# Dense tokens of layer 1 placed behind the last expert sum of layer 0

## What is computed

```python
for l in range(2):
    hn = rms_norm(h, norm_mix[l])
    if l == 0: y = gmlp_mix(hn, ...)                  # chunk token mixer
    else:      y = banded_attention(q, k_sh, v_sh) @ w_o   # 16 heads, shared K/V
    h = h + y
    hf = rms_norm(h, norm_ffn[l])
    h = h + peer_ffn(hf)      # 8 heads choose 16 of 16384 single-neuron experts per token
    if l == 0: k_sh, v_sh = split(rms_norm(h, norm_kv) @ w_kv)
return rms_norm(h, norm_final), ...
```

## Time and profile before

| | |
|---|---|
| median of 3 runs | 3456.22 us (3445.64 to 3458.19) |
| the profiled execution's own time | 3455.63 us |
| its span | 3453.5 us |
| PE, DVE busy | 3012.7 us (87%), 2514.5 us (73%) |
| DMA, whole span | 1043.13 MB, mean 302 GB/s |
| mean granted TensorE clock | 0.912 of full |

### The profile page before, as it was taken

The page is one execution under the profiler, slowest core; times in us unless marked ns, Lnnn a source line. Parts: engine busy times, 40 slices in busy tenths (PEclk is TensorE's granted clock), DMA queues, the critical chain, the costliest instruction groups (busy, mean ns, idle before and its releaser), DMA issues.

```text
span 3453.5 us, 46623 instructions
## 1 busy us (share of the span) xinstructions
PE 3012.7 (87%) x17310; PEld 2621.0 (76%) x17310; DVE 2514.5 (73%) x5433; ACT 808.9 (23%) x2386; POOL 1009.3 (29%) x840
## 2 busy tenths in 40 slices
PE   6899979999999997666688989799999999997565
PEld 6787868988888886555566857689888888885454
DVE  3377787777777778777633786988777777787777
ACT  3332212211111111111244452222111111111112
POOL 4431022222222223333254410122222222222332
PEclk9899989999999998777786978899999999998887
DMA  4225678999999999999521346679999999999996
GB/s 154 87 94 205 250 274 328 357 394 393 380 393 397 382 397 345 351 368 365 217 97 31 109 159 229 238 281 371 381 387 395 399 392 397 390 376 357 364 363 237
DMA packets 159975, 1043.13 MB, mean 302 GB/s; under 512 B 18480, under 2 KB 23920, under 8 KB 44096
## 3 DMA queue, kind: packets, MB, share of 16 engines
q0 software_dynamic: 92160, 671.13, 49.9%
q1 hardware_dynamic: 63648, 357.59, 27.5%
q10 hardware_dynamic: 4000, 12.36, 1.0%
HBM read 1033.28 MB, written 7.86 MB: 301 GB/s over the span
## 4 chain that ended last, share of the span: by engine, by line
DMA 35%; PE 32%; DVE 20%; issue 9%; ACT 1%; POOL 1%; SPq 0%; DVEq 0%; ACTq 0%; POOLq 0%
DMA gat<-uvg,idxg 35%; PE bank L695 9%; DVE acc L1568 9%; PE bank L499 7%; DVE gat L1560 3%; PE bank L486 3%; PE bank L488 3%; PE bank L487 3%; DVE oneA L1535 2%; PE bank L682 2%; DVE B L1541 2%; PE bank L584 1%; PE bank L516 1%; DVE E L1530 1%; PE bank L838 1%
## 5 line engine op out<-in xcount | busy, mean ns | idle before, releaser
L1245 POOL DMA_INDIRECT gat<-uvg,idxg x640 | 735.7, 1150 | 2074.3 <-DVE acc L1568 2005.9
L708 PE MATMUL bank<-a,V 128*128 128x256 f32 x4096 | 997.1, 406 | 216.8 <-DVE a L1552 216.6
L1560 DVE CUSTOM_DVE_ANT_0 gat<-gat,xrow 128x1024 f32<-128x1024 f32 x640 | 781.5, 1221 | 519.1 <-DMA gat<-uvg,idxg 514.8
L708 PEld LDWEIGHTS bank<-a,V 128*128 128x128 f32 x4096 | 837.3, 206 | 359.4 <-issue 230.1
L695 PE MATMUL bank<-xd,U 128*128 128x256 f32 x4096 | 926.1, 385 | 0.5 <-DMA U<-uvd 0.5
L695 PEld LDWEIGHTS bank<-xd,U 128*128 128x128 f32 x4096 | 780.4, 193 | 104.3 <-DMA U<-uvd 1.3
L1568 DVE SCALAR_TENSOR_TENSOR acc<-gat,wgt,acc 128x1024 f32<-128x1024 f32 x640 | 818.8, 1279 | 39.7 <-ACT wgt L1054 39.5
L1052 ACT ACTIVATE act<-dot 128x1 f32<-128x1 f32 x640 | 128.9, 201 | 1508.9 <-DVE dot L1560 1508.7
L682 PEld LDWEIGHTS bank<-B,oneA 128*128 128x128 f16 x4096 | 282.6, 150 | 34.0 <-DVE oneA L1535 19.4
L682 PE MATMUL bank<-B,oneA 128*128 128x32 f16 x4096 | 285.5, 246 | 19.7 <-DVE oneA L1535 17.6
L499 PE MATMUL bank<-xd,raw 128*128 128x256 f32 x1088 | 248.7, 386 | 7.5 <-DVE xd L1332 7.1
(11 more groups left out here) (192 smaller groups left out, 2278.3 us busy)
## 6 DMA issues: line engine op xcount, KB each, us to landing
U<-uvd SPq DMA_DIRECT2D x128, 1024.0 KB
V<-uvd SPq DMA_DIRECT2D x128, 1024.0 KB, 8.7
raw<-lin SPq DMA_DIRECT2D x152, 512.0 KB
gat<-uvg,idxg POOLq DMA_INDIRECT x640
hsp<-h ACTq DMA_DIRECT2D x2, 2304.0 KB, 13.9
hx<-hsp SPq DMA_DIRECT2D x2, 2304.0 KB, 13.9
sk_g<-skT ACTq DMA_DIRECT2D x2, 1024.0 KB, 4.9
sk_d<-skT ACTq DMA_DIRECT2D x2, 1024.0 KB, 8.1
```

Of the source, the lines that this page charges most:

```text
L708: mm = pe.matmul(bank[b][:, TD * (d % 2):TD * (d % 2) + TD], V[:, s, o:o + P], a[:, s, TD * k:TD * k + TD], start=(first and k == 0 and d ...
L1245: pool.indirect_dma_start(gat[:, s % SLOTS, :], None, uvg[l], bass.IndirectOffsetOnAxis(idxg[:, s:s + 1], 0)).then_inc(g_in[s % SLOTS], 16)
L1560: dve.tensor_tensor_reduce(gat[:, s % SLOTS, 0:D], gat[:, s % SLOTS, 0:D], xrow[:, min(s // P, 2), :], 1.0, 0.0, ALU.mult, ALU.add, dot[:, ...
```

## The change

The dense tokens' whole front part of layer 1 is moved ahead of the gathered tokens' part, and ahead of the end of layer 0's gather steps. Layer 0's pair loop ends with the sum of the dense tokens alone; then come their norm, K/V, queries, attention, output projection and best keys, with 34 gather steps of layer 0 among them (`TAIL`); `finish` then does the last multiply-add and the sum of the gathered tokens. Their norm, K/V and queries follow, with `choose` for the two dense chunks among them, then their attention and selection. Layer 1 thus begins its steps later: 40 stand ahead of its pairs. `step0` now puts `BOTH` = 170 steps into the first 40 pairs of each layer, and the rest (57 in layer 0, 110 in layer 1) into the last 24. The final norm is split in the same way. Buffers move with the order: keys and queries of the dense selection get places of their own (`sk_e`, `qs_e`), only the dense part of h is reloaded into `hx`, and `reload_h` brings back the gathered part.

```diff
@@ tables
-    [*[(f"att{n}", 1) for n in range(1, 16, 2)], *[(f"add{m}", 1) for m in range(6)],
-     *[(f"top{m}", 1) for m in range(8, HP)],
-     ("sel2", 2), ("sel3", 3), ("sel4", 3), *[(f"hot{m}", 2) for m in range(LEAD)]])
+    [("sel3", 3), ("sel4", 3), *[(f"hot{m}", 2) for m in range(LEAD)]])
+TAIL = ([("kv", 4), ("q", 8), *[(f"att{n}", 1) for n in range(1, 16, 2)], *[(f"od{m}", 1) for m in range(6)],
+         *[(f"top1{m}", 1) for m in range(8, HP)]], [])
+LATE = tuple(sum(n for _, n in a) for a in TAIL)
+BOTH = 170
@@ step0
-            return EARLY[l] + i * (NSTEP - EARLY[l]) // NPAIR
+            both = NPAIR - RING
+            if i <= both:
+                return EARLY[l] + i * BOTH // both
+            return EARLY[l] + BOTH + (i - both) * (NSTEP - EARLY[l] - LATE[l] - BOTH) // RING
@@ scalar
+            def keys_values(grp):
+                for m in range(4):
+                    act.wait_ge(*tile_done(f"kv{grp}", m))
+                    act.activation(kvs[:, m, COLS[grp]], bank[m][:, 0:SIZE[grp]], ACT.Copy).then_inc(free[m], 1)
+                    if grp == "g":
...
+                    else:
+                        weights_at(0, "kv" if m == 3 else "")
...
+            keys_values("d")
+            queries("d")
+            weights_at(0, "q")
+            act.wait_ge(attn_in, 16 * 2)
+            attention("d")
@@ vector
+            normed("n3d", G_KV, "d")
+            steps_at(0, "kv")
+            for b in range(4):
+                dve.wait_ge(*tile_done("kvd", b))
+            normed(None, G_MIX1, "d")
+            steps_at(0, "q")
+            values("d")
+            dve.wait_ge(attn_in, 16 * 2)
+            attention("d")
+            add_to_h(1, "od")
+            normed("n4d", G_FFN1, "d")
+            step = best_keys(1, "d", step)
+            finish(0)
+            normed("n3g", G_KV, "g", "kv")
+            step = choose(1, 0, step)
+            for b in range(4):
+                dve.wait_ge(*tile_done("kvg", b))
+            normed(None, G_MIX1, "g", "mix1")
+            step = choose(1, 1, step)
+            for c in DC:
+                take(1, c)
+            values("g")
             attention("g")
             add_to_h(1, "og")
             normed("n4g", G_FFN1, "g", "ffn1")
-            normed(None, G_MIX1, "d")
             step = best_keys(1, "g", step)
-            step = choose(1, 0, step)
-            attention("d")
-            add_to_h(1, "od")
-            normed("n4d", G_FFN1, "d")
-            step = choose(1, 1, step)
-            step = best_keys(1, "d", step)
             for i in (2, 3, 4):
                 step = choose(1, i, step)
                 steps_at(1, f"sel{i}")
             experts(1)
```

More of the change, by code:

```diff
@@ L129, in plan @@
     chosen_d(0)
+    seg("gt0", b4=1, b5=1)
+    rank(0, 3)
+    rank(0, 4)
     peer(0)
     norm("n3d")
+    lin("kvd")
+    lin("qd")
+    seg("vnd", b6=1, b7=1)
+    seg("attd", **{f"b{b}": 8 for b in range(8)})
+    lin("od")
+    norm("n4d")
+    chosen_d(1)
+    fin(0)
     norm("n3g")
-    lin("kvd")
+    seg("gt1", b4=1, b5=1)
+    rank(1, 0)
+    rank(1, 1)
     lin("kvg")
     lin("qg")
-    seg("vn", b6=3, b7=2)
+    seg("vng", b6=2, b7=1)
     seg("attg", **{f"b{b}": 12 for b in range(8)})
@@ L140, in plan @@
     chosen_g(1)
[L141 to L146, removed]
+    for i in (2, 3, 4):
+        rank(1, i)
     peer(1)
     norm("n5d")
+    fin(1)
     norm("n5g")
@@ L319, in gate_block, with placed @@
             return Wr[:, :, i, :, :] if j % 2 else Wr[:, i, :, :, :]
[L321 to L327, removed]
+        def placed(l, place):
+            for s, places in ((0, AT[l]), (NSTEP - LATE[l], TAIL[l])):
+                for p, n in places:
+                    if p == place:
+                        return range(s, s + n)
+                    s += n
             return range(0)
@@ L726, in experts @@
                     n += 2
-                for i in range(n, RING0):
+                for i in range(n, RING0 - 1):
                     expert_scores(l, i, i % 2)
@@ L1010, in selection @@
                     for m in range(HP - 3, HP):
-                        weights_at(l, f"top{m}")
+                        weights_at(0, f"top{l}{m}")
             def weights_at(l, place):
-                for s in early(l, place):
+                for s in placed(l, place):
                     weight(l, s)
@@ L1612, in _, with values @@
+            def values(grp):
+                for c in CHUNKS[grp]:
+                    b = 6 + c % 2
+                    dve.wait_ge(full[b], BASE[f"vn{grp}"][b] + 1 + (c == 4))
+                    dve.tensor_copy(vnat[0:TCS[c], c, :], bank[b][0:TCS[c], 0:KVH * DH]).then_inc(free[b], 1)
+                for b in (6, 7):
+                    dve.wait_ge(free[b], BASE[f"vn{grp}"][b] + 1 + (grp == "g" and b == 6))
+                dve.nop().then_inc(vnat_done, 1)
             step = 0
```

362 lines of the change are left out of this document (195 added, 167 removed).

## The result

The changed kernel took 3487.43 us (median of 4 runs, 3482.83 to 3492.86) against 3455.92 of the kernel before: a ratio of 1.0098, with a 95% interval of 1.0073 to 1.0122. It is slower by about 1%, 31.5 us. The profiled execution took 3487.5 us, so its stretches can be set against those of the earlier trace rows, whose execution took 3455.6.

The account below looks back on a forecast made before the run. It took PE and DMA as level in the first 40 pairs, gather steps and their bytes as limiting the last 24. Terms 18 - 131 + 51 + 5 + 26 + 38 + 3 = +10 on 3455.6 gave 3466 us, range 3412 to 3503.

Parts of the forecast that it names:

- The exposed steps: Between the loops: 12 of the 34 moved steps not hidden, costing 9 us ahead of dense queries and 21 behind them.
- Layer 0, first 40 pairs: Layer 0's first 40 pairs: 7 more steps priced by bytes at 389 GB/s, +18 us, bounds 0 and +25.
- Layer 1, first 40: Layer 1's first 40 pairs: 10 more steps priced by bytes at 393 GB/s, +26 us, bounds 0 and +30.
- from them alone I take 393 as full: First 40 pairs: trace rows with DMA 0.99 busy were read as a ceiling of 393 GB/s.
- PE's own need, 648: Layer 0's first 40 pairs: PE itself needs 648 us, so hides none of the added bytes if the rate stays.
- The fast rival: First 40 pairs: DMA has room left; at 410 GB/s both added terms vanish, giving 3422 us; chance 0.2.
- Layer 0, last 24: Layer 0's last 24 pairs: steps fall from 98 to 57, 376 us becomes 245, -131 us, bounds -151 and -100.
- The slow rival: Layer 0's last 24 pairs: not set by bytes; 12 us a pair, 288 us instead of 245, total 3509; chance 0.25.
- Between the loops: Layer 0's last multiply-add to layer 1's gathered best keys: 515.6 us becomes 567, +51, bounds +30 and +65.
- Ahead of layer 1's pairs: Stretch before layer 1's pair loop: two more gathered `choose` waits, less two steps and other small work, +5 us.
- End: Behind the last multiply-add: the dense and gathered norm chains follow each other instead of overlapping, +3 us.
- Layer 1, last 24: Layer 1's last 24 pairs: 14 more steps, +38 us by bytes at 353 GB/s; upper bound +53 counted by steps.

Follow-up runs that it names:

- e9_add_first: Changed kernel with DVE doing the multiply-add of the step before first, then the next step's dot product: 3384.1 us, 0.9813 of the kernel before.
- e12_before_add_first: Kernel before the change, with only the multiply-add put ahead of the next dot product on DVE: 3396.5 us, 0.9840 of the kernel before.
- e1_weights_spread: Changed kernel with ACT making one weight behind each K/V or query tile's copy, instead of four and eight behind the last: 3459.5 us.
- e6_ends: Changed kernel with weights spread behind tile copies, 160 steps in the first 40 pairs and three more step placements: 3432.4 us, 0.9926 of the kernel before.
- e3_both_160: Changed kernel with 160 instead of 170 gather steps in the first 40 pairs of each layer: 3467.1 us, 1.0040 of the kernel before.
- e7_both_150: Changed kernel with 150 instead of 170 gather steps in the first 40 pairs of each layer: 3536.2 us, 1.0227 of the kernel before.

## Why the prediction was right or wrong

The time fell in the range (3487 in 3412 to 3503), on the slow side of the main forecast's 3466, and by the prediction's own line of 0.5% the change is slower. The exposed steps and their reason were right. What sets the first 40 pairs was wrong, and two misses elsewhere, -10.2 and -11.1 below, took back half of what the other misses added (42.8). Without them the time would have been about 3509, outside the range: that it fell inside is in part luck.

- *Layer 0, first 40 pairs*: +18 forecast, +26.5 measured. *Layer 1, first 40*: +26, and +40.4. This is the step that failed: "from them alone I take 393 as full", and the price per step that follows, 2.7 us. e9_add_first shows 408 GB/s in the same stretch with the same steps, so the DMA engines were not full at 393. Above PE's floor of 630 us a step cost 3.9 to 4.0 us, a fourth of the cycle of its slot. The upper bounds, 25 and 30, were priced by bytes and too low, and the rate did not stay but fell (389 to 382, 393 to 385). "PE's own need, 648" was wrong too: with the same steps layer 0's first 40 pairs take 633.0 in e12_before_add_first, with PE busy throughout; the 647.95 held 3906 matmuls against 3822 there, more than 40 pairs' work. By their own working the two terms are 18.9 and 26.8; the sum has 18 and 26.
- *The fast rival* was right that there was room and wrong about what followed. It put the turn at 410 GB/s; 408 was reached, but only once the order on DVE was changed. It fell because the DMA engines' rate was not the limit.
- *Layer 0, last 24*: -131, measured -141.2: 380 GB/s, where the 245 us stand for 358. The slow rival (12 us a pair) fell: 9.8. PE's clock rose from 0.78 to 0.93 as it waited less.
- *Between the loops*: 567, measured 575.6. The two pauses were 8.8 and 22.5 (forecast 9 and 21), the dense queries 29.7 (29), dense attention to norm 100.0 (100). Mis-sized was the first block: from the last multiply-add to the end of K/V 32.4 instead of 24, because DVE waited 7.1 us for the sums of the norm and K/V took 16.6 instead of 14.0, both on PE at a granted clock of 0.68 and 0.77 after it had idled. The later blocks missed by less and cancel: `finish` 22.3 (20), gathered K/V to best keys 278 (285). e1_weights_spread confirms the order of ACT's list as the cause of the pauses.
- *Ahead of layer 1's pairs*: +5, measured +1.3. *End*: +3, measured +7.8: the two chains follow each other entirely.
- *Layer 1, last 24*: +38 by bytes, +48.2 measured. The bound by steps (+53) was the nearer one, and for the reason now known: 413.3 us / 114 steps = 3.6 us a step. With the multiply-add first the same pairs, up to the last sum, take 360.7 instead of 391.2.
- *Start*: 0, measured -11.1. The prediction gave it no term; some 6 are the granted clock of this one profile and 4.5 the earlier hot weights.
- *Signs*: DMA's share was to stay at 0.98 or more in the first 40 pairs; in layer 0 it was 0.97.

Sum of the misses: 8.5 + 14.4 - 10.2 + 8.6 - 3.7 + 4.8 + 10.2 - 11.1 = +21.5, the 21 us between 3466 and 3487.

The Trainium skill, "DMA: Bandwidth & Descriptors", section "Measured", gives 425 GB/s for a single core's 16 MB transfer. No run here reached it over a stretch; e9_add_first sustains 408 over 631 us, which leaves 425 standing and refutes my 393 as a ceiling. Taken as the whole story it would have given 3422, an estimate that was farther off than the one with the wrong 393, because the limit lay in neither.

Left open: why an execution has 8.1 or 14.2 us for the same matmuls in the start, and what made the median of e6_ends miss its theory. A fifth slot, the other way to shorten the cycle, was not tried: the memory map has no room for it.

## What to carry to other kernels

A busy DMA (0.98) at a steady rate is not proof of a full one: where a ring of buffers feeds it, read the cycle of a slot from the trace (from one fill of it to the next: issue, landing, wait for its reader's turn, release), divide it by the number of slots, and compare it with the bytes' time, before you price moved work by bytes. Release a buffer before you wait for the next one: that swap of two lines was worth 1.6% here, more than all the moving of steps. Where work is moved into another engine's list, look at what stands ahead of its smallest member (here a weight behind eight copies), and put it between them.

## What the runs showed of the hardware that was not expected

The DMA engines' busy share barely distinguishes rates: 392 GB/s at 0.99 (e3_both_160), 408 at 1.00 (e9_add_first), 377 at 0.97 (e7_both_150), all in the same stretch with the same sizes of transfer. The highest mean over such a stretch, 408 GB/s with 1 MiB gathers and 1 MiB loads side by side, came only when a slot was refilled without waiting for the next landing. Gathers nearly alone drew less: behind the last sum of e6_ends the dot products start at 3349.4, 3352.5, 3355.6, 3358.5 and 3361.1 us, 2.9 apart. That is 358 GB/s for the gathers and 384 with what else moved, at a share of 1.00; with four slots in their old order it says nothing of the limit.

A gather's issue on POOL took 0.94 us (median of 640) in the changed kernel and 1.68 in e9_add_first, the same instruction; the reason is open.

The same 48 matmuls took 8.1 or 14.2 us in executions of kernels with the same front part, at a mean granted clock of 0.90 or 0.73 between 100 and 150 us. So a difference in one stretch of one profile needs the granted clock beside it, and a timed run, before it is believed.
